# Mean squares of queries and keys from two rounded parts, issued at the end of each period

## The reference, cut to what matters

```python
def rms_norm(x, gain):
    xf = x.astype(jnp.float32)
    y = xf * lax.rsqrt(jnp.mean(xf * xf, axis=-1, keepdims=True) + EPS)
    return (y * gain.astype(jnp.float32)).astype(x.dtype)
...
    for g, (window, dilation) in enumerate(ATTN_GROUPS):
        q = rms_norm(proj[:, :, g, 0], q_gain[g]) * scale
        k = rms_norm(proj[:, :, g, 1], k_gain[g])
        o, lse = dilated_window_attention(q, k, proj[:, :, g, 2], window, dilation)
```

## Time and profile before

| | |
|---|---|
| Median of 3 runs | 2552.47 us |
| Lowest and highest run | 2548.88 and 2555.78 us |
| Profiled execution, own time | 2552.58 us |
| Its span in the profile | 2550.8 us |
| PE busy | 2353.2 us, 92% |
| PEld busy | 1541.0 us |
| DVE busy | 857.9 us, 34% |
| ACT busy | 535.5 us, 21% |
| POOL busy | 964.5 us, 38% |
| Granted clock, mean | 0.975 |

### The profile page before, as it was taken

The page is one execution under the profiler, slowest core; times in us unless marked ns, Lnnn a source line. Parts: engine busy times, 40 slices in busy tenths (PEclk is TensorE's granted clock), DMA queues, the critical chain, the costliest instruction groups (busy, mean ns, idle before and its releaser), DMA issues.

```text
span 2550.8 us, 27144 instructions
## 1 busy us (share of the span) xinstructions
PE 2353.2 (92%) x11369; PEld 1541.0 (60%) x11369; DVE 857.9 (34%) x1272; ACT 535.5 (21%) x1135; POOL 964.5 (38%) x462
## 2 busy tenths in 40 slices
PE   7999999999999999998999998899889888898987
PEld 5777787888887876765678886443324334343432
DVE  3764844555302027644414463111111111111012
ACT  3253542211102025666311102000000000000001
POOL 6545665888876762111178885000000000000000
PEclk9999999999999999999999998899999999999998
DMA  5212223322222321111023336699999999999995
GB/s 168 83 50 67 68 99 116 99 91 93 98 99 85 99 83 34 50 67 34 17 83 99 99 125 272 253 428 428 428 428 427 427 428 428 428 428 428 429 427 247
DMA packets 129027, 531.60 MB, mean 208 GB/s; under 512 B 6962, under 2 KB 89099, under 8 KB 103691
## 3 DMA queue, kind: packets, MB, share of 16 engines
q1 hardware_dynamic: 127467, 524.50, 51.8%
q10 hardware_dynamic: 1440, 5.37, 0.6%
HBM read 525.66 MB, written 4.19 MB: 208 GB/s over the span
## 4 chain that ended last, share of the span: by engine, by line
PE 74%; DMA 15%; DVE 6%; ACT 2%; issue 1%; POOL 1%; ACTq 0%; POOLq 0%; DVEq 0%
DMA arena<-in_w_exp_up 11%; PE ps L1420 7%; PE ps L1422 7%; PE ps L1421 7%; PE ps L2129 7%; PE ps L2102 7%; DMA ring<-in_w_exp_up 5%; PE ps L1740 5%; PE ps L2060 2%; PE ps L1512 2%; PE ps L1438 2%; PE ps L1436 2%; PE ps L1437 2%; PE ps L1514 1%; PE ps L1513 1%
## 5 line engine op out<-in xcount | busy, mean ns | idle before, releaser
L518 POOL TENSOR_TENSOR w_lo<-ring,w_hi 128x1024 fp32r<-128x1024 f32 x222 | 548.0, 2469 | 227.9 <-ACT w_hi L625 212.5
L515 POOL TENSOR_TENSOR w_hi<-ring,one 128x1024 fp32r<-128x1024 f32 x196 | 383.6, 1957 | 384.2 <-PE ps L1422 97.1
L2102 PE MATMUL ps<-ring,arena 128*64 128x512 f32 x944 | 346.9, 608 | 35.5 <-DMA arena<-in_w_exp_up 20.7
L2102 PE MATMUL ps<-arena 128*64 128x512 f32 x944 | 350.7, 615 | 27.7 <-DMA arena<-in_w_exp_up 11.9
L582 POOL TENSOR_TENSOR arena<-arena 128x512 f32<-128x512 f32 x8 | 8.4, 1049 | 800.6 <-PE ps L2072 781.6
L1420 PE MATMUL ps<-h_hi,w_hi 128*128 128x512 f32 x624 | 243.1, 390 | 0.0
L1422 PE MATMUL ps<-h_hi,w_lo 128*128 128x512 f32 x624 | 242.9, 389 | 0.0
L1421 PE MATMUL ps<-h_lo,w_hi 128*128 128x512 f32 x624 | 242.8, 389 | 0.0
L2102 PEld LDWEIGHTS ps<-ring,arena 128*64 128x64 f32 x944 | 109.1, 140 | 189.9 <-issue 188.0
L2102 PEld LDWEIGHTS ps<-arena 128*64 128x64 f32 x944 | 110.8, 141 | 150.5 <-issue 150.5
L930 ACT ACTIVATE arena<-ps 64x1024 f32<-64x1024 f32 x32 | 30.8, 1009 | 550.3 <-PE ps L2102 550.3
(11 more groups left out here) (339 smaller groups left out, 4227.9 us busy)
## 6 DMA issues: line engine op xcount, KB each, us to landing
ring<-in_w_exp_gate SPq DMA_DIRECT2D x33, 2048.0 KB, 33.9
arena<-in_w_exp_up SPq DMA_DIRECT2D x33, 2048.0 KB, 30.2
arena<-in_w_exp_gate SPq DMA_DIRECT2D x26, 2048.0 KB, 34.9
ring<-in_w_exp_up SPq DMA_DIRECT2D x26, 2048.0 KB, 30.4
ring<-in_w_exp_down SPq DMA_DIRECT2D x26, 2048.0 KB, 30.4
arena<-in_w_exp_down SPq DMA_DIRECT2D x26, 2048.0 KB, 31.9
ring<-in_w_in SPq DMA_DIRECT2D x34, 1024.0 KB, 5.1
ring<-in_ffn_w_up SPq DMA_DIRECT2D x22, 1024.0 KB, 5.1
```

The lines of the kernel that those rows point to most:

```text
L515: nc.gpsimd.tensor_tensor(hi, w, one[:].unsqueeze(2).to_broadcast(list(w.shape)), ALU.mult).then_inc(w_high, 1)
L518: nc.gpsimd.tensor_tensor(lo, w, hi.bitcast(f32), ALU.subtract).then_inc(w_split, 1)
L2102: last = mm(ps[64 * i:64 * i + 64, c, :], xeT[:, k, a * CAP:(a + 1) * CAP], w[:, c * 512:c * 512 + 512], start=(k == 0), stop=(k == KT - 1))
```

## The change

The squares are rounded by ScalarE into `sq_hi`, VectorE subtracts to get the rest in `sq_lo`, and the mean is two products, of each part with a rounded copy `mean_r` of the averaging matrix, added up in PSUM (1/64 is exact when rounded). `mean_r` is written by ScalarE before its first norm. In the periods of the attention the mean is issued last, behind the value products and the last projection part, and it waits for the subtraction.

```diff
--- before.py
+++ after.py
@@ -125,6 +125,9 @@
         br_lo = part("br_lo", arena_at, 8192, KT, S)
         mg_hi = part("mg_hi", arena_at, 0, KT, S)
         mg_lo = part("mg_lo", arena_at, 27136, KT, S)
+        sq_hi = part("sq_hi", arena_at, 16384, 2, S)
+        sq_lo = part("sq_lo", arena_at, 17408, 2, S)
+        mean_r = part("mean_r", arena_at, 31104, P)
 
 
 
@@ -229,6 +232,7 @@
+        sq_high, sq_low = sem("sq_high"), sem("sq_low")
@@ -636,6 +640,8 @@
                 if n >= 2:
                     act.wait_ge(ssq_ps, n - 1)
                 A(sq[:, n % 2, :], ps[:, 4 + n % 2, :], F.Square).then_inc(sq_done, 1)
+                act.wait_ge(sq_done, n + 1)
+                A(sq_hi[:, n % 2, :], sq[:, n % 2, :], F.Copy).then_inc(sq_high, 1)
 
             def root(n):
 
@@ -650,6 +656,7 @@
                 A(mk_new[:, j, :], ps[:, 4 + j % 2, 0:MEM], F.Copy).then_inc(mk_ev, 1)
 
             act.wait_ge(consts, 1)
+            A(mean_r, mean64[:], F.Copy)
             norm(0, x, junk0, lambda t: (in_x[t], 16))
             act.wait_ge(vec_done, 1)
             norm_hi(0, h_hi, MIXG, S)
@@ -996,6 +1003,9 @@
                     o, a = o.rearrange("p (c j) -> p j c", c=4), a.rearrange("p (j c) -> p j c", c=4)
                 dve.wait_ge(sq_done, n + 1)
                 V.tensor_copy(o, a).then_inc(qr_done, 1)
+                dve.wait_ge(sq_high, n + 1)
+                V.tensor_tensor(sq_lo[:, n % 2, :], sq[:, n % 2, :], sq_hi[:, n % 2, :].bitcast(f32),
+                                ALU.subtract).then_inc(sq_low, 1)
 
             def scaled(n):
 
@@ -1522,8 +1532,9 @@
                     pe.wait_ge(v_ev, TT * g + 3 + b)
                 else:
                     pe.wait_ge(rt_done, n - 1)
-                pe.wait_ge(sq_done, n + 1)
-                mm(ps[:, 6 + n % 2, :], mean64[:], sq[:, n % 2, :], start=True, stop=True).then_inc(ssq_ps, 1)
+                pe.wait_ge(sq_low, n + 1)
+                mm(ps[:, 6 + n % 2, :], mean_r, sq_hi[:, n % 2, :], start=True, stop=False)
+                mm(ps[:, 6 + n % 2, :], mean_r, sq_lo[:, n % 2, :], start=False, stop=True).then_inc(ssq_ps, 1)
 
             def mk_part(j, half):
 
@@ -1649,8 +1660,6 @@
                         last.then_inc(t_ps, 1)
                     for f in todo[1:2]:
                         fill(g, f)
-                    for n in ended(g, i, "qk"):
-                        mean_sq(n)
                     m = u - 2
                     if i >= 2:
                         _, p, tiles = units[m]
@@ -1668,6 +1677,8 @@
                         last.then_inc(pv_done, 1)
                     for f in todo[2:]:
                         fill(g, f)
+                    for n in ended(g, i, "qk"):
+                        mean_sq(n)
 
             def coefs(b):
```

## The result

The changed kernel takes 2562.34 us (median of 6 runs, 2556.91 to 2562.71) against 2553.49 for the kernel before in the same set (6 runs). The ratio is 1.0028, 95% interval [1.0017, 1.0039]: slower by 0.28%, and above the range that I gave.

A forecast was written before the change was run, and what follows sets the result against it. TensorE bounds most stretches, a ScalarE and VectorE loop 167 to 201 us. Terms -2.4 -2.4 +0.65 -0.8 -1.8 +3.3 +1.25 +1.5 = -0.7 us, from 2552.58 to 2551.9; range 2545.0 to 2559.5.

The forecast's parts named there:

- The stall at 94 to 112 us: Blocks 0 to 7: VectorE has slack; mean 6 gives nothing, subtraction 7 delays GpSimd's second half, +0.65 us.
- group 1: Attention periods 255 to 300 us: VectorE needs 7.65 us against TensorE's 8.05, so it does not set the pace.
- slower rival: Subtraction and scaling both meet GpSimd each period of 255 to 300 us, VectorE needs 10.05: +9.3, about 2561; chance 0.17.
- The start: First 21 us: earlier table load and scalings win turns against GpSimd, -2.4 us, bounds 0 and -4.3.
- The means: Two rounded products replace one float32 product: 0.40 us saved each outside the attention periods, 0.20 inside.
- The loop: ScalarE and VectorE loop, 160 to 205 us: four turns lengthened by the subtraction, +3.3 us, bounds 0 and +6.4.
- The step at 208 us: Between groups 0 and 1: subtraction 14 waits for GpSimd and mean 14 for it, +1.25 us, bounds 0 and +1.6.
- The step at 305 to 318 us: Between groups 1 and 2: two more subtractions ahead of block 23's scaling, +1.5 us, bounds -0.9 and +3.5.
- Behind 350 us: After the changed code: nothing differs but the start, no term.

The follow-up runs named there:

- a4: Changed kernel without VectorE's subtraction, both products of a mean reading the rounded squares (low part left out); ratio 0.9963 to the kernel before.
- d1: Changed kernel with the subtraction replaced by a second VectorE copy of the block from PSUM, ahead of the raw copy; ratio 0.9979 to the kernel before.
- b2: Changed kernel with copies and subtractions computed but unused, the mean one float32 product at its new place; ratio 1.0037 to the kernel before.
- a2: Kernel before with only the copy of the averaging matrix added ahead of ScalarE's first norm; median 2552.91 us, ratio 0.9982.
- a3: Changed kernel with the copy of the averaging matrix moved behind the evictions of v; median 2564.81 us, ratio 1.0031 to the kernel before.
- a1: Changed kernel again, unaltered, in a second set of runs; median 2562.08 us, ratio 1.0022 to the kernel before.
- d3: Kernel before plus the matrix copy at the start and the two parts for blocks 0 to 4 and 16 to 22 only; ratio 0.9982.
- d2: Kernel before with only the float32 means of the periods moved behind the value products; ratio 0.9983.
- b1: Kernel before again, unaltered, for a second profile; ratio 1.0001.
- f1: Kernel before plus matrix copy at the start, period means last in their period, two parts for blocks 0 to 4 only; 2546.36 us, ratio 0.9968.
- b3: Changed kernel with the means of the periods back at their old place, ahead of the value products; ratio 1.0034 to the kernel before.
- b4: Changed kernel with the two parts in blocks 0 to 7 only, the others with the old float32 mean at its old place; ratio 1.0004.
- c1: Changed kernel with the subtraction replaced by a VectorE copy of one SBUF tile (low part left out); ratio 1.0006 to the kernel before.
- c2: Changed kernel with the two parts in blocks 8 to 23 only, the others with the old float32 mean at its old place; ratio 1.0015.
- c3: Changed kernel with the subtractions of blocks 8 to 23 behind mask and maximum on VectorE; ratio 1.0032 to the kernel before.
- e2: Kernel before plus matrix copy at the start and all period means last in their period, no parts anywhere; ratio 0.9981.

## Why the prediction was wrong

*The stall at 94 to 112 us: the step that failed.* I wrote "VectorE has slack, the raw copies wait for ScalarE" and priced the meetings there at +0.65 for one subtraction. Measured from 88 to 115 us: +4.2 and +5.7, where my own terms come to -0.15. I had set the period against TensorE's for group 1 (7.65 against 8.05) and for the rival (10.05), but never for the prologue, where the same sum gives 6.35 against 6.6 unmet and 9.8 met. TensorE's waits for VectorE there are 4.8 and 6.0 us in the two profiles, and half the clock for 3.4 us behind them, which I had priced at one place only (320 to 322 us). The mechanism of my slower rival was right and its place wrong; that its 2561 comes near the measured 2562.34 is luck. a4 and d1, without meetings, gain 0.8 there; b2 shows that it is the queue and not the mean's own wait.

*The start: right in kind, a little small.* -2.4 forecast; v began 3.1 us earlier by the medians of 16 and 4 profiles, a2 gives -4.0 and a3 against a1 2.4 to 2.7. At 50 us the first profile (-5.5), a4 (-5.0) and d3 (-4.8) are beyond my bound of -4.3: they began v at 18.8 to 19.1 us, and in the first the clock rose 2.9 us after it.

*The means.* Outside the periods 0.40 each, in a4 all six. Two records of 0.23 us in the chain of the changed kernel, for 0.86 in the earlier trace rows:

```profile
61.15 0.23 PE ps L1536
61.37 0.24 PE ps L1537
```

Inside the periods a little over 0.2 each: 233 to 292 us, five means, gives -1.3 in both profiles. VectorE did not bound group 1, as said.

*The loop: +3.3.* Taking out means 9 and 10 (-0.4), the first profile has +3.3 and a1 +5.0. The waits were as forecast; a1's 1.7 more is one stretch at half the clock, which I had not priced. My bounds of 0 and +6.4 held. A turn was 11.8 us, as said (changed kernel, chain of waits, table load to table load):

```profile
178.53 1.28 ACT L651
...
186.37 0.52 DVE sq_lo L1007
...
190.32 1.28 ACT L651
```

*The step at 208 us: wrong in sign.* +1.25 forecast, less 0.4 for mean 15; measured -0.6 and -1.0. The loop's lateness had moved subtraction 14 out of GpSimd's way (0.69 us), and the earlier value products gain by themselves (d2: -0.7).

*The step at 305 to 318 us.* +1.5 forecast; from 292 to 349 +2.1 and +0.9, where b1 has +1.3 with nothing changed. The number is near by luck. What I gave as one term hid two: the moved place takes 2.8 away (d2), the subtractions give it back and add a wait of the mean of 3.54 us:

```profile
308.43 0.76 PE L1536 MATMUL ps<-sq_hi,mean_r 128*128 128x512 f32 x1 [3.54 <-DVE sq_lo L1007]
```

*Behind 350 us: "nothing differs but the start".* The work does not, but the time does: +5.4 and +2.3 in the two profiles. It is not the change's work, for a2 has +5.7 there and d2 -1.4. The same code meets stretches at half the clock of other lengths in each execution: behind 349 us they come to 119.5 us in both profiles of before, to 139.9 and 129.7 in those of the changed kernel, and to 112.6 (f1) at the least. Two stretches, before and then after:

```profile
950.00:960.00 10.00, 5.44 (x17) 3.33 (x17) 2.77 (x7) 5.53 (x13) 2.38 (x1) 0.83 0.00 0
1280.00:1290.00 10.00, 7.88 (x35) 6.53 (x36) 2.75 (x4) 0.63 (x2) 2.84 (x3) 1.00 0.33 105
```
```profile
950.00:960.00 10.00, 4.37 (x13) 3.13 (x12) 4.29 (x13) 7.74 (x18) 1.95 (x1) 0.68 0.00 1
1280.00:1290.00 10.00, 7.81 (x22) 5.01 (x21) 2.79 (x4) 3.22 (x5) 3.44 (x2) 0.83 0.31 105
```

Over the 19 profiles of the table this part runs from -1.4 to +6.4 us, middle value +3.6; it goes with the time at half the clock (correlation 0.83, 0.29 us for each us more). The profile that I made my sum against was one of the quick ones: I wrote that its median of three was 2552.47, "so no correction", but the later medians of before were 2554.6 to 2556.9 in sets of 12 to 31 runs.

In sum: to 349 us I forecast -0.7. The two profiles of the changed kernel have +0.6 and +4.8, mean +2.7; the two of before 0 and -2.1, mean -1.1: +3.8 between them, a miss of 4.5, and the stall alone is 4.3 to 5.8 us above what I had for it. The sets of runs say +5.2 and +8.9. What is left, 1.4 to 5.1 us, lies behind 349 us. The runs' own clocks say that a part of it is the changed kernel's: their mean is 0.9694 in the 11 runs of a1 and 0.9718 in the 23 of before beside them, some 12 us more at half the clock, of which the profiles have 7 from 40 to 349 us. By an estimate from these numbers that leaves 5 us more behind 349, worth about 1.5. Why the same code behind 349 us should be at half the clock for longer stays open; the profiles alone would not show it, since a3, b2, b3, b4, c1, c2 and c3, all with a late VectorE, drift by +0.5 to +6.4 there, a2 and d3 by +5.7 and +3.8.

## What to carry to other kernels

Before adding an operation to an engine, add up that engine's period in each stage, once unmet and once with every operation that can meet another engine at its met length, and compare it with the period of the engine that sets the pace; here one stage with some 0.3 us of slack decided. A copy from PSUM could be added here where a copy or subtraction between SBUF tiles could not. And before forecasting a few us, take a second profile of the unchanged kernel: here two of them differed by 3.4 us in the first 50.

## What the hardware did that I had not expected

- A copy from one SBUF tile to another on VectorE met GpSimd like a subtraction of two (400 ns alone, up to 2425), a copy from PSUM of the same size never did (668 to 693 in 24).
- The clock rose 2.9 to 6.1 us after TensorE's first long run of products began, in executions whose work up to there was the same.
- A float32 mean took 0.86 us to the next product between rounded products, 0.95 at its old place in a period and 1.06 at the new one, between float32 operations (before and d2), so moving an unchanged product changed its price; still the move paid, by where the scalings then fell.
- A wait of TensorE could cost twice: in the changed kernel's first profile the clock fell to 0.50 for 3.4 us behind a wait of 2.67 us at 96 us. In d2, e2 and f1, where no wait from 40 to 349 us is longer than 1.7, it did not fall at all there. It is no rule: behind the same wait of 1.38 us for GpSimd it fell in b1 (222 us) and stayed at 1.00 in the first profile of before (225 us).
- Half the clock can cost nothing: that stretch of b1 left its shift at -3.4, because TensorE, slower, no longer had the next wait for GpSimd (1.09 us in the first profile of before).
